# Around the joined pair of chunks in the feed-forward blocks: row sums, down weights and loads in another order

## What is computed

```
D_MODEL = 1024; SEQ = 256; D_FF = 2816
def swiglu_ffn(h, w_gate, w_up, w_down):
    return (jax.nn.silu(h @ w_gate) * (h @ w_up)) @ w_down
...
        h = rms_norm(x, norm_pre[l, 0])
        x = x + 0.5 * rms_norm(swiglu_ffn(h, ffn1_w_gate[l], ffn1_w_up[l], ffn1_w_down[l]), norm_post[l, 0])
```

## Time and profile before

| what | value |
|---|---|
| median of 3 runs | 2059.15 us (2056.28 to 2060.22) |
| the profiled execution | 2059.28 us, span of its instructions 2057.5 us |
| PE busy | 2011.0 us, 98% of the span |
| DVE busy | 1542.2 us, 75% |
| ACT busy | 1257.8 us, 61% |
| transfers | 394.55 MB, mean 192 GB/s |

### The profile page before, as it was taken

The page is one execution under the profiler, slowest core; times in us unless marked ns, Lnnn a source line. Parts: engine busy times, 40 slices in busy tenths (PEclk is TensorE's granted clock), DMA queues, the critical chain, the costliest instruction groups (busy, mean ns, idle before and its releaser), DMA issues.

```text
span 2057.5 us, 24287 instructions
## 1 busy us (share of the span) xinstructions
PE 2011.0 (98%) x9442; PEld 1644.1 (80%) x9442; DVE 1542.2 (75%) x1892; ACT 1257.8 (61%) x1570; POOL 0.2 (0%) x4
## 2 busy tenths in 40 slices
PE   8999999999999999999999999999999999999998
PEld 6778887888787778887888788888887887888877
DVE  6776899777857776899767857876677578666774
ACT  6555657665657556667565656756656557566554
POOL 0000000000000000000000000000000000000000
PEclk9999999999999999999999999999999999999999
DMA  7756774567667755764567666554675674636654
GB/s 259 228 184 195 215 200 148 169 195 209 210 192 231 218 186 174 235 192 145 176 198 205 199 193 206 196 155 150 194 221 182 188 229 162 177 135 196 209 192 125
DMA packets 339123, 394.55 MB, mean 192 GB/s; under 512 B 123824, under 2 KB 235072, under 8 KB 339008
## 3 DMA queue, kind: packets, MB, share of 16 engines
q1 hardware_dynamic: 334912, 381.94, 60.4%
q10 hardware_dynamic: 4096, 11.05, 1.5%
HBM read 365.66 MB, written 1.05 MB: 178 GB/s over the span
## 4 chain that ended last, share of the span: by engine, by line
PE 79%; DVE 8%; DMA 4%; ACT 4%; issue 3%; SPq 2%; ACTq 0%; DVEq 0%
PE ps L738 68%; PE ps L875 4%; DMA raw<-in_ffn_w_up 2%; DVE w_lo L2112 2%; ACT w_hi L1420 1%; PE ps L809 1%; DVE scratch L2529 1%; ACT scratch L1527 1%; PE ps L1360 1%; SPq L567 1%; PE ps L1341 1%; DMA raw<-in_w_up 0%; DVE x L2162 0%; SPq L531 0%; DVE scratch L2284 0%
## 5 line engine op out<-in xcount | busy, mean ns | idle before, releaser
L2112 DVE TENSOR_TENSOR w_lo<-raw,w_hi 128x2048 fp32r<-128x2048 f32 x336 | 766.0, 2288 | 196.1 <-ACT w_hi L1420 194.0
L1420 ACT ACTIVATE w_hi<-raw 128x2048 fp32r<-128x2048 f32 (+2 forms) x340 | 642.9, 1897 | 392.8 <-PE ps L738 172.9
L738 PE MATMUL ps<-w_hi,hT_hi 128*128 128x512 f32 x1856 | 731.4, 394 | 0.0
L738 PE MATMUL ps<-w_lo,hT_hi 128*128 128x512 f32 x1856 | 723.5, 390 | 0.0
L738 PE MATMUL ps<-w_hi,hT_lo 128*128 128x512 f32 x1856 | 699.4, 389 | 0.0
L738 PEld LDWEIGHTS ps<-w_hi,hT_hi 128*128 128x128 f32 x1856 | 349.0, 188 | 76.0 <-issue 5.7
L738 PEld LDWEIGHTS ps<-w_hi,hT_lo 128*128 128x128 f32 x1856 | 348.4, 188 | 73.4
L738 PEld LDWEIGHTS ps<-w_lo,hT_hi 128*128 128x128 f32 x1856 | 349.1, 188 | 69.3
L738 PE MATMUL ps<-w_hi,bT_hi 128*128 128x512 f32 x608 | 240.1, 395 | 7.0 <-DVE bT_lo L2203 7.0
L738 PE MATMUL ps<-w_hi,bT_lo 128*128 128x512 f32 x608 | 237.0, 390 | 0.0
L738 PE MATMUL ps<-w_lo,bT_hi 128*128 128x512 f32 x608 | 236.8, 390 | 0.0
(11 more groups left out here) (340 smaller groups left out, 1755.7 us busy)
## 6 DMA issues: line engine op xcount, KB each, us to landing
raw<-in_w_in SPq DMA_DIRECT2D x160, 512.0 KB, 4.7
raw<-in_ffn_w_down SPq DMA_DIRECT2D x88, 512.0 KB, 4.4
raw<-in_ffn_w_gate SPq DMA_DIRECT2D x86, 512.0 KB, 4.1
raw<-in_ffn_w_up SPq DMA_DIRECT2D x86, 512.0 KB, 5.0
raw<-in_w_gate SPq DMA_DIRECT2D x44, 512.0 KB, 4.0
raw<-in_w_up SPq DMA_DIRECT2D x44, 512.0 KB, 5.0
raw<-in_w_down SPq DMA_DIRECT2D x44, 512.0 KB, 4.4
raw<-in_w_out SPq DMA_DIRECT2D x32, 512.0 KB, 4.2
```

What stands on the lines that cost most here:

```text
L738: mm = nc.tensor.matmul(bank(t, half), act[:, tiles[i], t * P:(t + 1) * P], w, start=start and (i, n) == steps[0], stop=stop and (i, n) == ...
L1420: nc.scalar.activation(dst, src, ACT.Copy).then_inc(high_ready, 1)
L2112: V.tensor_tensor(lo, src, flat(hi), ALU.subtract).then_inc(low_ready, 1)
```

## The change

Four moves, all inside the FFN code, all in the order of things that are done anyway; no instruction is added or taken out.

- DVE, chunk 4 (the one ahead of the pair): `row_sums_low` stands ahead of the low part of the activations of chunk 3, and the low part of p5's weights ahead of `hidden(4)` and `part(4)`.
- ACT, in the pair: the conversion of down4's weights stands ahead of the joining of chunk 4's halves.
- ACT and DVE, chunk 7 (behind the pair): on ACT the joining of chunk 6 stands ahead of the conversion of gu(8,0)'s weights; on DVE the low part of chunk 5's activations ahead of that of down6's weights.
- SP, chunk 8: the load of gu(8,0) stands ahead of the transposes of chunk 6.

```diff
@@ SP @@
                 if c - 3 in PAIRS:
                     turn_halves(L, n, c - 3)
+                gate_up(L, k0 + AT["gu", c, 0], 0, wg, wu, c)
+                if c - 3 in PAIRS:
                     turn_halves(L, n, c - 2)
-                gate_up(L, k0 + AT["gu", c, 0], 0, wg, wu, c)
@@ ACT, chunk_behind @@
                 high(L, k + 3)
                 hidden(c - 2)
+                hidden(c - 1, second_hi)
                 if ahead:
                     form_high(c + 1, 1)
                 else:
                     high(L, k + 4)
-                hidden(c - 1, second_hi)
@@ ACT, pair @@
                 hold(held_5, 5, 5)
+                high(L, k0 + AT["down", c - 1])
                 multiplied(L, k0 + AT["down", c - 2])
                 hidden(c - 1)
-                high(L, k0 + AT["down", c - 1])
@@ DVE, chunk @@
                 ahead = c + 1 in PAIRS
+                if c + 1 == PAIRS[0]:
+                    row_sums_low()
                 join(c - 1)
                 if not ahead:
                     weight_low(L, k + AHEAD)
                 hidden_low(c - 1)
...
-                if c + 1 == PAIRS[0]:
-                    row_sums_low()
                 if ahead:
                     t1(c + 1)
                     weight_low(L, k + AHEAD)
-                else:
-                    weight_low(L, k + 1 + AHEAD)
+                weight_low(L, k + 1 + AHEAD)
                 hidden(c)
                 part(c)
-                weight_low(L, k + (1 if ahead else 2) + AHEAD)
+                if not ahead:
+                    weight_low(L, k + 2 + AHEAD)
@@ DVE, chunk_behind @@
                 join(c - 2)
+                hidden_low(c - 2)
                 weight_low(L, k + 3)
-                hidden_low(c - 2)
```

## The result

| what | before | changed |
|---|---|---|
| median | 2057.72 us (4 runs, 2054.05 to 2060.22) | 2023.63 us (4 runs, 2023.48 to 2025.26) |
| ratio | | 0.9838, 95% interval 0.982 to 0.9855 |
| profiled execution | 2059.28 us | 2023.48 us |
| mean granted clock | 0.995 | 1.0 |

The changed kernel is 34.1 us faster by the medians and 35.8 us by the profiled executions. The runs also lie closer together: within 1.8 us instead of 6.2.

The account below looks back on a forecast made before the run. PE, busy 98% of the span, was taken as the bound, losing time to waits and low clock. Gains of 9.8, 4.5, 3.5, 14.3 and 8.5 us, less 0.5 and 1.2, give 38.9 off 2059.28: 2020.4 us, range 2016 to 2033.

Parts of the forecast that it names:

- Case (a): The forecast itself: all four moves gain as summed, 2020.4 us, own range 2016 to 2024, chance 0.74.
- Move 1 and 2: DVE ahead of the pair ends p2's waits, 9.8 us less 0.5; ACT in it ends down4's, 4.5 less 1.2.
- The rest of 0.2 us at down4: Down4's start hangs on p5's end, so 0.2 us of waiting stays in all six FFNs, 1.2 us.
- p2's raw weights as the new limit of t4: DVE's t4 needs p2's load, landing at 516.68; p2's low part still ends with 1.0 us to spare.
- Move 3: DVE behind the pair: chunk 5's low part ahead of down6's weights ends down5's six waits, gain 3.5 us.
- Move 4: ACT and SP behind the pair: down6's wait for chunk 6's low part goes, gain 14.3 us, 1.1 to spare.
- Rival (b): Chunk 6's transposes land later behind gu(8,0)'s load, down6 still waits 1.4 us per FFN: 2034 us, chance 0.12.
- (c): Down6 waits for something other than ACT's order and its wait stays whole: 2041.5 us, chance 0.06.
- (d): Slower: ACT stands before late chunk 6 transposes, holding gu(8,0)'s conversion and chunk 7's silu: 2083 us, chance 0.04.
- (e): No change: the weights' loads set the pace and PE waits later for what it gains: 2059 us, chance 0.04.
- One sign of being wrong: ACT idle for more than 3 us before the second joining (chunk 6's) would speak for the late-transposes or slower rival.
- The clock: Five pieces of PE at 1.2 GHz behind long waits, 1.7 us each, go with their waits: 8.5 us.

Follow-up runs that it names:

- e1: The kernel before with only the DVE moves ahead of the pair (row sums and p5's low part earlier): 2059.18 us, ratio 1.0003 to before.
- e2: The kernel before with only the ACT move in the pair (down4's conversion ahead of chunk 4's joining): 2052.96 us, ratio 0.9975 to before.
- e3: The kernel before with the DVE moves ahead of the pair and the ACT move in it: 2046.71 us, ratio 0.9944 to before.
- e5: The changed kernel with SP's order of before (both chunks' transposes, then gu(8,0)'s load): 2023.34 us, ratio 0.9828 to before.
- e7: The changed kernel with DVE's order of before behind the pair (down6's weights, then chunk 5's low part): 2027.10 us, ratio 0.9843 to before.
- e4: The kernel before with only the three moves behind the pair (ACT, DVE, SP): 2035.69 us, ratio 0.9892 to before.
- e11: The changed kernel with both ACT's and SP's order of before behind the pair: 2050.05 us, ratio 0.9959 to before.
- e6: The changed kernel with ACT's order of before behind the pair (gu(8,0)'s conversion, then chunk 6's joining): 2023.74 us, ratio 0.9829 to before.
- e9: The changed kernel with the row sums again behind hidden_low(3), p5's low part staying ahead: 2028.36 us, ratio 0.9851 to before.
- e12: e5 plus, in the first FFN, p7's load ahead of chunk 3's transposes and t1 ahead of hidden_low(3): 2020.90 us, ratio 0.9814 to before.

## Why the prediction was right, and where it was off

The time was forecast at 2020.4 us with 2016 to 2033 as range; it is 2023.63. Case (a) came true, at the upper end of its own range of 2016 to 2024.

- **Move 1 and 2 belong together**, with down4's start as what counts: shown by e1, e2 and e3. The rest of 0.2 us at down4 is there: it starts at 520.50, 0.38 us behind the matmul before it and not 0.23, which with the 0.08 behind its first matmul is 0.23. The list of waits does not show it, because the overlap of 0.16 us hides so small a wait. It was forecast for all six FFNs and stands in four: in the first the step is 0.28 us and in the fourth 0.23, since PE comes late from p2 there.
- **p2's raw weights as the new limit of t4**: shown, by the 0.49 us of t4's wait for that load. The 1.0 us to spare is not always enough: in the fourth FFN t4 waited 1.62 us for the load and p2 started 0.28 us late (0.51 instead of 0.23 behind the matmul before it), and in e5 and e7 p2's wait there is in the list, 0.37 and 0.31. That is the late load for which 0.2 us were left.
- **Move 3**, 3.5 us: e7 measured 3.5 by the medians.
- **Move 4**: the wait goes, and its cause was ACT's order behind gu(8,0)'s load (e4, e11). The transposes did land later behind the load, with the second joining starting 4.1 us before down6 in the second FFN where 4.0 were worked out (559.9 less 555.9). What the prediction did not say is that SP's move and ACT's are each enough alone (e5, e6). Rival (b) had the mechanism right and the size wrong; (c), (d) and (e) are out. One sign of being wrong did appear and meant nothing: ACT idles 3.4 to 3.8 us before the second joining in 11 of the 12 places of the two traces. The sign was set too low. By the forecast's own numbers ACT has joined chunk 5 by 552.3 and gets chunk 6 at 555.9, 3.6 us later.
- **The clock**: five pieces, 8.5 us, gone. That they hung on the waits is shown by the traces (last section), that each costs 1.7 us is worked out from the granted clock alone. The first FFN's piece went although 1.70 us of its wait stayed. That it went was partly luck, since a wait of 1.82 us at the same place was followed by a piece in e9.

**The term that was mis-sized** is the remainder of p2's wait in the first FFN. "In the first FFN the shift of 2.9 against a wait of 3.1 leaves 0.3": it left 1.70. The prediction looked at p2's load as limit of t4 and not at p7's as limit of t1, which stood there too: in the first FFN it landed at 82.1, and so the 2.4 us that the row sums had freed were cut to 0.8 (t1 at 82.22 instead of 82.97). e12 shows it. In the five other FFNs of the changed kernel t1 waits for that load too, 0.57 to 1.30 us, but there PE is not held by it; in the fifth FFN of e6 it was, where t1 waited 2.55 us and p2 0.58. With the modelled end this is 1.7 us of the difference. A second one, which the prediction put at nothing, is down5's wait of 0.61 in the second FFN, 0.85 us, in one of two traces. Taken off the sum of 38.9, they leave 36.4; the profiled executions differ by 35.8. The 0.6 us between are not placed: at 91 us, ahead of p2, the changed kernel is 0.07 us behind, and by the waits of later stages each FFN's gain falls short of its own sum by 0.2 us at most. By the medians the gain is 34.1, mostly because that of the kernel before fell from 2059.15 to 2057.72 with its fourth run.

## What to carry to other kernels

An engine that takes its instructions in order makes everything behind a wait late: look at what stands behind the longest wait for a load, and ask whether it needs that load. Where two waits of the bound engine follow each other, find the chain that fixes the later one before you count the earlier; taken away alone it may be worth nothing, and both together more than their sum. And count waits that are long enough to be followed by low clock at more than their length: here 1.7 us on top of some 2, behind about half of them.

## What the runs showed of the hardware

- Behind the program's first microseconds, low clock stands only at waits of the engine's own, and not at each. In the 14 traces of this study PE had 38 waits of 1.9 us or more in the FFNs, and 22 of them were followed or ended by a piece at 1.2 GHz; of the 25 waits between 1.0 and 1.9 us one was, of 1.82 us. The same wait of down6 (2.0 to 2.3 us) had a piece behind it in four of six FFNs in one trace and in two of six in another (e2, where p2's wait of 3.15 us in the first FFN had none either). The Trainium skill (TensorE: Matmul & The Clock Gate, Part 1) has windows that run freely, and by that rule the number should vary from run to run; the traces agree, and so does the spread of the runs, 6.2 us with the waits and 1.8 without. The spread follows the clock: of the nine runs of the kernel before timed beside e9 to e12, those of 2056.3 to 2057.2 us have a mean granted clock of 0.997, and those of 2060.9 and 2061.2 us 0.994.
- Chunk 6's two transposes, issued behind two loads of 512 KB, landed 3.7 to 5.3 us after their issue in both traces of the changed kernel, and 2.3 to 2.4 where they had the queue to themselves: 0.4 to 1.1 us behind the loads, in all six FFNs. In the five other traces with SP's move they landed 3.8 to 5.4 us after their issue.
